# Transposes moved into the gate and up product of an expert, and the second expert moved ahead of the routing table

## The reference

```
scores = sigmoid(x @ router_w)                       # 64 experts
_, idx = top_k(scores + router_bias, 8)
wsel   = sel / sum(sel) * 2.5
gates  = sum(one_hot(idx, 64) * wsel)
hid    = silu(x @ exp_w_gate[e]) * (x @ exp_w_up[e])     # 256 wide, each expert
routed = (hid * gates[..., None]) @ exp_w_down[e]        # summed over experts
shared = (silu(x @ shared_w_gate) * (x @ shared_w_up)) @ shared_w_down
x      = x + g_f * (routed + shared)
```

## Time and profile before

| what | value |
|---|---|
| median of three runs | 789.59 us |
| profiled execution, span from its first to its last instruction | 787.9 us |
| PE busy | 696.4 us, 88% |
| VectorE, ScalarE, POOL busy | 42%, 29%, 38% |
| bytes moved by DMA | 279.22 MB, mean 354 GB/s |

### The profile page before, as it was taken

One profiled execution on the slowest core, in us unless ns is written; L12 is line 12 of the kernel. 1 busy time (PEld: TensorE's weight loads), 2 busy tenths in 40 slices (PEclk: granted clock), 3 DMA queues, 4 the chain that ended last, 5 costly groups with the idle time before them and its releaser, 6 DMA issues.

```text
span 787.9 us, 15116 instructions
## 1 busy us (share of the span) xinstructions
PE 696.4 (88%) x5157; PEld 396.9 (50%) x5158; DVE 328.4 (42%) x615; ACT 228.1 (29%) x391; POOL 300.1 (38%) x315
## 2 busy tenths in 40 slices
PE   3999999999999999999999999998789967987930
PEld 3666657446655555455555555544445534543510
DVE  3163658378154443444324333333333433342217
ACT  4132603033133321123313232232322322232212
POOL 0050112021326554345544463556444644455120
PEclk9999999999999999999999999999999999999975
DMA  8996899945669999999999999999999999999843
GB/s 321 416 332 240 342 384 374 377 161 232 255 221 385 380 411 415 370 392 393 400 380 395 386 395 404 384 411 396 408 413 393 403 397 417 401 401 401 358 103 129
DMA packets 60139, 279.22 MB, mean 354 GB/s; under 512 B 18926, under 2 KB 20218, under 8 KB 32693
## 3 DMA queue, kind: packets, MB, share of 16 engines
q1 hardware_dynamic: 36520, 252.35, 79.1%
q0 software_dynamic: 23136, 25.28, 13.4%
q10 hardware_dynamic: 428, 0.87, 0.3%
HBM read 272.54 MB, written 26.30 MB: 379 GB/s over the span
## 4 chain that ended last, share of the span: by engine, by line
PE 70%; DMA 20%; DVE 5%; issue 2%; ACT 1%; SPq 1%; POOL 0%; POOLq 0%; DVEq 0%; ACTq 0%
PE bank L1153 28%; DMA gu<-in_exp_w_up 18%; PE bank L1189 13%; PE bank L884 5%; PE bank L866 4%; PE bank L1014 4%; PE bank L1129 3%; PE bank L854 2%; PE bank L1170 2%; PE bank L925 1%; DMA gu<-in_mix_w 1%; PE bank L887 1%; PE bank L1245 1%; PE bank L1098 1%; PE bank L1125 1%
## 5 line engine op out<-in xcount | busy, mean ns | idle before, releaser
L1153 PE MATMUL bank<-gu,et 128*64 128x256 f32 x2480 | 282.7, 380 | 29.6 <-DMA gu<-in_exp_w_up 25.1
L1153 PEld LDWEIGHTS bank<-gu,et 128*64 128x64 f32 x2480 | 180.3, 137 | 147.9 <-issue 70.9
L551 POOL DMA_INDIRECT acc_rows<-et,idx x64 | 104.7, 1635 | 239.5 <-DVE et L1682 132.0
L1189 PE MATMUL bank<-dn,et 128*64 128x512 f32 x632 | 149.7, 602 | 12.5 <-issue 10.3
L1675 DVE COPY et<-bank 128x256 f32<-128x256 f32 x64 | 27.1, 424 | 251.6 <-PE bank L1170 251.6
L745 ACT ACTIVATE et<-bank 64x512 f32<-64x512 f32 x64 | 37.8, 591 | 257.7 <-PE bank L1153 257.7
L1189 PEld LDWEIGHTS bank<-dn,et 128*64 128x64 f32 x632 | 40.4, 136 | 79.4 <-issue 79.4
L755 ACT ACTIVATE et<-bank,mb 128x512 f32<-128x512 f32 x64 | 44.0, 687 | 121.1 <-PE bank L1189 102.2
L1682 DVE TENSOR_SCALAR et<-bank,mb 128x512 f32<-128x512 f32 x64 | 48.0, 751 | 68.5 <-PE bank L1189 57.5
L1668 DVE TENSOR_TENSOR et<-et 64x512 f32<-64x512 f32 x64 | 67.8, 1060 | 0.4 <-ACT et L746 0.4
L561 POOL DMA_DIRECT2D small<-halfc x49 | 55.9, 1141 | 0.0
(11 more groups left out here) (294 smaller groups left out, 626.3 us busy)
## 6 DMA issues: line engine op xcount, KB each, us to landing
dn<-in_exp_w_down SPq DMA_DIRECT2D x64, 1024.0 KB, 23.0
gu<-in_exp_w_up SPq DMA_DIRECT2D x63, 1024.0 KB, 23.4
gu<-in_exp_w_gate SPq DMA_DIRECT2D x62, 1024.0 KB, 19.7
gu<-in_ada_rest SPq DMA_DIRECT2D x5, 2048.0 KB, 9.8
gu<-in_mix_w SPq DMA_DIRECT2D x4, 2048.0 KB, 12.4
mb<-in_ada_rest SPq DMA_DIRECT2D x3, 2048.0 KB, 11.6
gu<-in_lru_in_w SPq DMA_DIRECT2D x4, 1024.0 KB, 14.5
gu<-in_sgu_in_w SPq DMA_DIRECT2D x2, 2048.0 KB, 13.1
```

The source lines that it names most:

```text
L551: pool.indirect_dma_start(acc_rows[u % 2], bass.IndirectOffsetOnAxis(ap=idx[:, u, 0:1], axis=0), yo[:, u % 2, 0, :], None, bounds_check=2 ...
L1153: mm = pe.matmul(bank[u % 2][64 * c:64 * c + 64, b * FE:(b + 1) * FE], xt[:, b, k % 4, k // 4, :], w[c][:, k * FE:(k + 1) * FE], start=(k ...
L1189: mm = pe.matmul(bank[5 + b][64 * c:64 * c + 64, :], hT[:, b, j, :], dn[:, dslot(u), j * D + c * HALF:j * D + (c + 1) * HALF], start=(j == ...
```

## The change

The product of an expert is cut in two on PE. `gate_up_head` has its waits, the second block if there is one, and the first five k tiles of the first block; `gate_up_rest` has the last three k tiles and raises `gu_done`. Between them stand `turn_h` of e - 1 and `turn_x` of e + 1. `down` of e - 1 follows behind the rest. The turned tokens get a second home, so that those of e + 1 can be written while the rest of e still reads its own: even experts use the old buffer, odd ones free parts of `xT` and `mb`. ScalarE copies its half (`xt1`) ahead of `gates` instead of behind them. The whole table (three batches) stands behind expert 1's product; in `one_hots` the gate factors of batch 2 are written last instead of ahead of the one-hots. No matmul, copy or DMA is added or taken away.

```diff
+HEAD = 5
...
-        xt = part(1024).rearrange("p (s k h n) -> p s k h n", s=2, k=4, h=2)
+        xt_lo = part(1024)
...
+        xt_f = [[xt_lo[:, 0:512], xt_lo[:, 512:1024]], [xTf[:, KT * FE:KT * T], mbf[:, 3184:3696]]]
+        xt = [[h.rearrange("p (k h n) -> p k h n", k=4, h=2) for h in b] for b in xt_f]
...
             def body(r, i, first=False, last=False):
                 for u in range(U):
+                    if not (last and u == U - 1):
+                        xt1(r, i + (u + 1) // U, (u + 1) % U)
                     gates(r, i, u)
...
-                    if not (last and u == U - 1):
-                        xt1(r, i + (u + 1) // U, (u + 1) % U)
...
+            def products(r, i, u, b, ks):
...
+                for k in ks:
+                    for c in range(2):
+                        mm = pe.matmul(bank[u % 2][64 * c:64 * c + 64, b * FE:(b + 1) * FE], xt[u % 2][b][:, k % 4, k // 4, :],
+                                       w[c][:, k * FE:(k + 1) * FE], start=(k == 0), stop=(k == KT - 1))
+                return mm
+
+            def gate_up_head(r, i, u, full):
...
                 with pe.If(full):
-                    blocks(1)
-                blocks(0).then_inc(s["gu_done"], 1)
+                    products(r, i, u, 1, range(KT))
+                products(r, i, u, 0, range(HEAD))
+
+            def gate_up_rest(r, i, u):
+                products(r, i, u, 0, range(HEAD, KT)).then_inc(s["gu_done"], 1)
...
                 for u in range(V):
-                    gate_up(r, i, u, now)
+                    after = None if last and u == V - 1 else is_full(r, i + (u + 1) // V, (u + 1) % V)
...
-                    if first and r == 0 and u == 0:
-                        table(0, 0)
-                        table(0, 1)
-                    if first and r == 0 and u == 1:
-                        table(0, 2)
+                    gate_up_head(r, i, u, now)
                     if before is not None:
                         turn_h(r, i if u else i - 1, (u - 1) % V, before)
+                    if after is not None:
+                        turn_x(r, i + (u + 1) // V, (u + 1) % V, after)
+                    gate_up_rest(r, i, u)
+                    if first and r == 0 and u == 1:
+                        for h in range(3):
+                            table(0, h)
...
-                        turn_x(r, i + (u + 1) // V, (u + 1) % V, after)
                     if before is not None:
                         down(r, i if u else i - 1, (u - 1) % V, before)
...
-                if h == 2:
-                    dve.wait_ge(s["tb_mm"], TOP * r + 3)
-                dve.tensor_tensor(mv(r, h)[:, :, :, :, 1], mk[:, a:b], over_k(gpart, n), ALU.mult).then_inc(s["mv_gate"], 1)
+                if h < 2:
+                    dve.tensor_tensor(mv(r, h)[:, :, :, :, 1], mk[:, a:b], over_k(gpart, n), ALU.mult).then_inc(s["mv_gate"], 1)
...
+                if h == 2:
+                    dve.wait_ge(s["tb_mm"], TOP * r + 3)
+                    dve.tensor_tensor(mv(r, h)[:, :, :, :, 1], mk[:, a:b], over_k(gpart, n), ALU.mult).then_inc(s["mv_gate"], 1)
```

More of the change, by code:

```diff
@@ L737, in xt1 @@
                 act.wait_ge(s["xt_ready"], r * NE + i * U + u + 1)
[L738 removed]
+                act.activation(xt_f[u % 2][1], bank[3][:, :], ACT.Copy).then_inc(s["xt1_evac"], 1)
             def gates(r, i, u):
@@ L1130, in turn_x @@
                 mm.then_inc(s["xt_ready"], 1)
-            def gate_up(r, i, u, full):
+            def products(r, i, u, b, ks):
                 e = r * NE + i * V + u
-                special = isinstance(e, int) and e == SLOTS
-                sl = gslot(e, u)
-                if special:
+                w = [guf[gslot(e, u)][:, c * KT * FE:(c + 1) * KT * FE] for c in range(2)]
+                if isinstance(e, int) and e == SLOTS:
+                    w = [xTf, late]
+                if isinstance(e, int) and e == SLOTS + 1:
+                    w[0] = gmodf
+                for k in ks:
[4 more added lines that the diff above has]
+            def gate_up_head(r, i, u, full):
+                e = r * NE + i * V + u
+                if isinstance(e, int) and e == SLOTS:
                     pe.wait_ge(ld_shared_gu, 48)
                 elif isinstance(e, int) and e < SLOTS:
-                    pe.wait_ge(ld_gu[sl], 32)
+                    pe.wait_ge(ld_gu[gslot(e, u)], 32)
                 else:
-                    pe.wait_ge(ld_gu[sl], 8 * (e - 1 - (u - 1) % SLOTS) + 32)
+                    pe.wait_ge(ld_gu[gslot(e, u)], 8 * (e - 1 - (u - 1) % SLOTS) + 32)
                 pe.wait_ge(s["xt0_evac"], e + 1)
@@ L1145, in gate_up @@
                     pe.wait_ge(s["up_evac"], e - 1)
-                w = (xTf, late) if special else (guf[sl], guf[sl][:, KT * FE:2 * KT * FE])
-                if isinstance(e, int) and e == SLOTS + 1:
-                    w = (gmodf, w[1])
-                def blocks(b):
-                    for k in range(KT):
-                        for c in range(2):
-                            mm = pe.matmul(bank[u % 2][64 * c:64 * c + 64, b * FE:(b + 1) * FE], xt[:, b, k % 4, k // 4, :],
-                                           w[c][:, k * FE:(k + 1) * FE], start=(k == 0), stop=(k == KT - 1))
-                    return mm
                 with pe.If(full):
-                    blocks(1)
-                blocks(0).then_inc(s["gu_done"], 1)
+                    products(r, i, u, 1, range(KT))
+                products(r, i, u, 0, range(HEAD))
+            def gate_up_rest(r, i, u):
+                products(r, i, u, 0, range(HEAD, KT)).then_inc(s["gu_done"], 1)
             def turn_h(r, i, u, full):
@@ L1202, in body @@
                 for u in range(V):
-                    gate_up(r, i, u, now)
+                    after = None if last and u == V - 1 else is_full(r, i + (u + 1) // V, (u + 1) % V)
                     half = i * V + u - SHARED_AT if r == 0 and isinstance(i, int) and 0 <= i * V + u - SHARED_AT < 6 else None
-                    if first and r == 0 and u == 0:
-                        table(0, 0)
-                        table(0, 1)
-                    if first and r == 0 and u == 1:
-                        table(0, 2)
+                    gate_up_head(r, i, u, now)
                     if before is not None:
                         turn_h(r, i if u else i - 1, (u - 1) % V, before)
+                    if after is not None:
[4 more added lines that the diff above has]
+                            table(0, h)
                     if half is not None and half % 2 == 0:
                         shared_turn(half // 2)
-                    after = None
-                    if not (last and u == V - 1):
-                        after = is_full(r, i + (u + 1) // V, (u + 1) % V)
-                        turn_x(r, i + (u + 1) // V, (u + 1) % V, after)
                     if before is not None:
@@ L1660, in xt0 @@
                 dve.wait_ge(s["xt_ready"], r * NE + i * U + u + 1)
-                dve.tensor_copy(xt[:, 0].rearrange("p k h n -> p (k h n)"), bank[2][:, :]).then_inc(s["xt0_evac"], 1)
+                dve.tensor_copy(xt_f[u % 2][0], bank[2][:, :]).then_inc(s["xt0_evac"], 1)
             def hidden(r, i, u):
```

1 line of the change is left out of this document (removed).

## The result

The changed kernel took **792.29 us** (median of 20 runs, 788.11 to 794.81), the kernel before 790.08 us (20 runs, 786.1 to 793.23): a ratio of **1.0029, interval 1.0016 to 1.0043**. Forecast were 787.9 us and a range of 785.0 to 790.6. Measured again later on another chip, beside three experiments, the same two kernels gave 790.56 (12 runs) and 790.05 us (35), a ratio of 1.000 (0.9975 to 1.0025). So the change costs between nothing and 0.4%, and what was forecast to be gained was not gained. The profiled executions span 792.3 and 787.9 us.

A forecast was written before the change was run, and what follows sets the result against it. The prediction took the DMA queue of weight loads as the bound, full to the end. Gains of 0.8 us (head) and 0.9 us (end), 1.7 us in all, off the 789.59 us median gave 787.9 us, range 785.0 to 790.6.

The forecast's parts named there:

- In 240 to 740 us I cost all of this at 0: Expert loop: weight buffers freed 0.86 us later cost nothing, since the queue of loads covers it.
- cover of 3.0 us: Expert loop: the queue of loads is at least 8.2 - 5.2 = 3.0 us deep, from landing times.
- Rival 3: Light experts to 330 us: transposes wait for gathers, 6.9 us late, 3.9 us dry queue, 792.6 us; chance 0.10.
- 0.5 us an expert: Rival 3's assumed PE loss to gather waits, over the dozen light experts to 330 us.
- The head: Start, experts 0 to 2: DMA hole cut in four, 7.6 against 7.3 us; gain -0.3 to 2.4, taken 0.8 us.
- The tail: After the last wait for weights: a 0.24 us gap and 0.69 us of issue go, 0.9 us gained.
- untouched: End of the kernel: the scatters and the final norm were forecast not to change.
- Rival 1: Head: expert 6's weights come 5.1 us sooner and all of it is kept, 783.6 us; chance 0.12.
- Rival 2: PE sets the pace: its 6.2 us idle in 240 to 500 us counts, 781.3 us; chance 0.04.
- slower: Whole kernel: the outcome of a loss beyond the 0.3% bound, chance 0.08.
- within 0.3%: Whole kernel: the outcome of a change no larger than 0.3%, 2.4 us, chance 0.58.
- longer waits for weights: Expert loop, 240 to 740 us: the gaps that PE saves turn into longer waits for weights.

The follow-up runs named there:

- e3: Changed kernel with only the token transposes back behind the whole product (ScalarE's token copy behind `gates` too): 790.78 us, 1.0025 of the kernel before.
- e4: Changed kernel with only the routing table back in its old place, between experts 0 and 1: 791.18 us, 1.001 of the kernel before.
- HEAD = 2: Changed kernel with the transposes after two eighths of the product: 793.59 us; with gathers four experts ahead too, 791.6 us, 1.0037 of gathers ahead alone.

## Why the prediction was wrong

- **The failed step: "In 240 to 740 us I cost all of this at 0."** It counted 0.86 us of later release per expert against a cover of 3.0 us. The cover was about right: delays beyond some 3 us made the last weights late. The delay was mis-sized, because I left out what a wait *inside* the product does: load 24 went out 5.6 and 3.8 us later, not 0.86, and the last weights landed 2.7 and 0.9 us later, not 0.8 sooner. In the profile after, load 11 is 4.55 us late; the profile of before held both numbers needed, the wait at 267.51 and the load at 267.29 just ahead of it.
- **Rival 3's argument against itself failed.** It said that the loop of down product, scatter, gather and transposes is met by a faster PE, but not made slower. It is made slower: before, the down product follows the transposes at once (268.06 + 0.66 = 268.72); now the rest of the product stands between them (269.17 to 271.80). The change lengthens this loop by three eighths of a product, 1.29 us, and 2.63 where the clock was low. Its mechanism is what the traces show, and its price, 792.6 us, is near the first comparison's 792.29; that closeness is partly luck, since the second comparison gave 790.56, the delay was 5.6 us and not 6.9, and the queue was dry for 0.6 us and not 3.9. Its chance of 0.10 was too low. Its "0.5 us an expert" was wrong in shape: the waits are few and long (1.80, 3.04, 2.46 us).
- **The head: right in its times, its gain not shown.** Product and table ended within 0.6 us of the forecast, and the hole's sum stayed about the same, as forecast. In three profiles with gathers ahead the last weights came 1.1, 0.6 and 0.8 us sooner than before, about the 0.8 expected. The runs with the table back show 0.6 and 0.7 without the moved table, so the gain is not the table's; and it is no larger than the 1.2 us by which the kernel before scatters.
- **The tail: right.** 0.9 forecast, 1.07 measured, and the issue gaps before down products are gone. What lies behind that, the prediction left "untouched"; there the profile after lost 2.5 us, and whose they are stays open.
- **Rival 1 (783.6 us)** is out: the holes did not close. **Rival 2 (781.3 us)**, PE as the pace, is out: the gaps it would remove are removed where the gathers are ahead, and the time falls by 0.8 to 2.3 us below the kernel before, not 8. This is where the Trainium skill (Perfetto Trace Analysis, Identifying the Most-Contended Engine) leads if its word on occupancy is read alone. The same section judges DMA by HBM utilization and does not take matmul busy time for TensorE's distance from roofline, so these runs speak against that half reading and not against the section.
- The chance of "slower", 0.08, was also too low. Two comparisons put the change at 1.0029 and 1.000, so "within 0.3%" (0.58) was no foolish choice, but the profile showed an existing wait of 0.55 us at the very instruction that was moved ahead of other work, and that should have weighed more.

How far the time is explained: beside each other on one chip, the changed kernel with the gathers ahead takes 0.9964 (0.994 to 0.9993) of the changed kernel, while the kernel before gains nothing from the same edit (0.9999). That is the evidence that waits for gathers cost the changed kernel time. Against it stand e3 (slow without such waits), e4 (the same waits, last weights on time) and the 2.9 us of HEAD = 2 with gathers ahead. So that the loads go out late, and why, is shown; that this makes up the whole of the lost time is not.

What seems to beat both kernels: the changed one with gathers one expert further ahead, 788.92, 787.72 and 788.67 us in three series, against 789.98, 790.05 and 789.43 of before beside them; with the table back it is 787.79, the one interval (0.9958 to 0.9997) that excludes no gain. Some 0.1 to 0.3%.

## What to carry to other kernels

Before an instruction that waits is moved ahead of work on an in-order engine, list what will now stand behind its wait: here a buffer's release, a load and the step on which the next gather depends. A wait of half a microsecond at its old place is the warning, and the first thing to move is its producer: with the gathers an expert earlier the same change no longer lost. A full DMA queue forgave delays of some 3 us here and not more; shortest landing under load less landing alone (2.7 to 3.8 us in three profiles) gives about that size. The busy share is a weak sign of it: it still read 1.03 over the stretch in which the rate had fallen from 393 to 388 GB/s.

## What the runs showed that I had not expected

The granted clock. In the profile after, it stands at 0.5, the 1.2 GHz level, for short stretches that follow long waits of PE (1.9 to 3.3 us): seven between 200 and 745 us. The kernel before has none, two and one in its three profiles, though it too waits up to 3.5 us for weights. Two of the seven stand behind waits for gathers, the rest behind waits for weights, and the changed kernel with gathers ahead still has five in each of its three profiles. Windows of the kernel after: the wait for the gather, the stretch behind it, and the one behind that.

```profile
266.00:268.50 2.50, 0.00 (x0) 0.00 (x0) 0.07 (x1) 0.00 (x0) 2.20 (x3) 1.00 1.02 316
269.00:272.00 3.00, 3.00 (x16) 1.66 (x16) 0.69 (x1) 0.75 (x2) 1.02 (x2) 0.55 1.05 410
273.00:276.00 3.00, 3.00 (x26) 1.57 (x22) 1.74 (x2) 0.74 (x2) 0.24 (x1) 1.00 1.03 408
```

It makes a wait dearer than its length: the twelve matmul records of the rest took 2.63 us there and 1.45 at the 2.4 GHz level. Where PE has idle time anyway the clock eats into that first: in 500 to 740 us PE is busy 213.94 us against 207.73, 6.2 us more. Its waits for weights are 23.7 us (13 times, longest 3.3) against 25.1, and the gaps before down products, 4.7 us in that stretch before, are gone. The prediction expected these gaps to come back as longer waits for weights; that time went into slower matmuls instead.
